# A transformer layer's prologue: the first modulation part computed in columns, its loads and the bias table moved

## The reference

```python
mod = jax.nn.silu(c) @ w_ada[l] + b_ada[l]                 # c: (1, 1024), w_ada: (1024, 6144)
sh1, sc1, g1, sh2, sc2, g2 = jnp.split(mod, 6, axis=-1)
h = rmsnorm(x, pre_mix_gain[l]) * (1.0 + sc1[:, None]) + sh1[:, None]
y = token_mixer(h, w_in[l], ...)                           # proj = h @ w_in, w_in: (1024, 3072)
x = x + g1[:, None] * rmsnorm(y, post_mix_gain[l])
h = rmsnorm(x, pre_ffn_gain[l]) * (1.0 + sc2[:, None]) + sh2[:, None]
y = hier_moe(h, ...)                                       # 32 SwiGLU experts, two of them for each token
x = x + g2[:, None] * rmsnorm(y, post_ffn_gain[l])
```

## Time and profile before

| | us |
|---|---|
| Median of 3 runs | 787.15 (783.61 to 787.57) |
| The profiled execution: its own time | 786.79 |
| Its span in the profile | 785.1 |
| PE busy | 732.4 (93%) |
| DVE busy | 637.0 (81%) |
| ACT busy | 526.9 (67%) |
| HBM read | 248.30 MB, 318 GB/s over the span |

### The profile page before, as it was taken

How to read it: one execution, slowest core, us unless ns; L and a number is a source line. 1 busy time by engine, 2 the same in 40 slices (tenths; PEclk the granted TensorE clock), 3 DMA queues, 4 the chain that set the end, 5 groups by cost and what they waited for, 6 DMA issues and landing times.

```text
span 785.1 us, 12664 instructions
## 1 busy us (share of the span) xinstructions
PE 732.4 (93%) x4733; PEld 572.3 (73%) x4734; DVE 637.0 (81%) x539; ACT 526.9 (67%) x546; POOL 307.3 (39%) x214
## 2 busy tenths in 40 slices
PE   4769999989769999999999999999999999999994
PEld 1248577544557888888888888888888888888883
DVE  3364285645647999999999999999999999999995
ACT  2020133365526888888888888888888888888873
POOL 7400000040053444666444666444666544666000
PEclk9979999999658999999999999999999999999998
DMA  9999987720518899999999999999999999999901
GB/s 342 327 406 385 393 317 281 286 92 0 214 55 299 301 372 374 379 371 369 373 368 385 373 376 377 365 382 374 371 377 366 375 374 381 374 372 375 365 1 57
DMA packets 101997, 249.69 MB, mean 318 GB/s; under 512 B 8134, under 2 KB 8146, under 8 KB 98898
## 3 DMA queue, kind: packets, MB, share of 16 engines
q1 hardware_dynamic: 96448, 244.33, 84.1%
q10 hardware_dynamic: 5092, 3.46, 1.4%
q0 software_dynamic: 432, 1.59, 0.6%
HBM read 248.30 MB, written 1.07 MB: 318 GB/s over the span
## 4 chain that ended last, share of the span: by engine, by line
PE 85%; DVE 6%; DMA 4%; POOL 2%; ACT 2%; issue 1%; DVEq 0%; ACTq 0%; POOLq 0%
PE PS L1294 46%; PE PS L1282 7%; PE PS L1262 7%; PE PS L1253 6%; PE PS L1086 5%; PE PS L1204 4%; PE PS L1080 4%; POOL line L380 2%; DMA toe<-line_dram 2%; PE PS L1272 2%; DMA tabT<-in_rel_bias_dram 1%; DVE MOD L726 1%; PE PS L1061 1%; DMA line_dram<-line 1%; DVE S L802 1%
## 5 line engine op out<-in xcount | busy, mean ns | idle before, releaser
L946 DVE TENSOR_TENSOR WL<-W,WH 128x2048 fp32r<-128x2048 f32 x187 | 419.8, 2295 | 7.3 <-ACT WH L629 7.3
L629 ACT CAST WH<-W 128x2048 fp32r<-128x2048 f32 x187 | 349.9, 1904 | 48.5 <-PE PS L1294 48.5
L423 POOL TENSOR_SCALAR OG<-slot_no,cur 128x128 f32<-128x128 f32 x64 | 161.7, 2530 | 0.0
L1294 PE MATMUL PS<-WH,XT 128*128 128x512 f32 x512 | 139.9, 395 | 0.6 <-DVE XT L965 0.6
L1294 PE MATMUL PS<-WL,XT 128*128 128x512 f32 x508 | 139.9, 397 | 0.0
L410 POOL COPY cur<-PG 128x4 f32 (+1 forms) x33 | 8.3, 251 | 275.7 <-PE PS L1272 228.2
L1294 PEld LDWEIGHTS PS<-WH,XT 128*128 128x128 f32 x512 | 96.7, 189 | 23.6 <-DVE XT L965 0.6
L1294 PEld LDWEIGHTS PS<-WL,XT 128*128 128x128 f32 x508 | 96.0, 189 | 22.4
L420 POOL TENSOR_SCALAR OH<-slot_no,cur 128x128 bf16<-128x128 f32 x64 | 106.6, 1675 | 0.0
L726 DVE SCALAR_TENSOR_TENSOR MOD<-W,cS,MOD 128x2048 f32<-128x2048 f32 x20 | 47.0, 2349 | 29.6 <-DMA W<-in_w_ada_dram 29.3
L1294 PE MATMUL PS<-WH,HT 128*128 128x512 f32 x248 | 69.2, 401 | 1.5 <-issue 1.5
(11 more groups left out here) (198 smaller groups left out, 778.5 us busy)
## 6 DMA issues: line engine op xcount, KB each, us to landing
W<-in_w_gate_dram SPq DMA_DIRECT2D x64, 1024.0 KB, 8.0
W<-in_w_down_dram SPq DMA_DIRECT2D x64, 1024.0 KB, 6.0
W<-in_w_up_dram SPq DMA_DIRECT2D x63, 1024.0 KB, 9.9
W<-in_w_ada_dram SPq DMA_DIRECT2D x24, 1024.0 KB, 8.3
W<-in_w_in_dram SPq DMA_DIRECT2D x12, 1024.0 KB, 13.9
W<-in_w_out_dram SPq DMA_DIRECT2D x4, 1024.0 KB, 11.4
toe<-line_dram POOLq DMA_DIRECT2D x1, 1536.0 KB, 13.4
X<-in_x_dram ACTq DMA_DIRECT2D x1, 1024.0 KB, 12.4
```

The lines of the kernel that those rows point to most:

```text
L423: nc.gpsimd.tensor_scalar(OG[:, buf, t, :], slot_no[:], cur[:, buf, 0, t:t + 1], cur[:, buf, 1, t:t + 1], ALU.is_equal, ALU.mult).then_inc ...
L629: nc.scalar.copy(WH[:, (UPE * odd + u) % SPLITS, :], source).then_inc(hi_ready, 1)
L946: nc.vector.tensor_tensor(low, source, WH[:, (UPE * odd + u) % SPLITS, :].bitcast(f32), ALU.subtract).then_inc(lo_ready, 1)
L1294: last = nc.tensor.matmul(PS[:, bank, :], lhsT, w[:, q * 512:(q + 1) * 512], start=begin, stop=end)
```

## The change

The first modulation part is loaded as 8 other units ("first", part, j): four with the 1024 scale columns (rows 256j to 256j+255, two row blocks side by side), then four with the 1024 shift columns. All four units of the projection's blocks 0 and 1 follow sooner: no later modulation units stand ahead of block 0, two stand between blocks 1 and 2, behind them come three, three, four and four.

The results of the first part are kept in columns: `scol` and `shcol` hold one value for each of 8x128 channels, in the partition of the channel. DVE multiplies 1024 columns at a time (`first`). The sum over the partitions is made on PE with a piece of 128 columns of `MOD` as weights and one column of ones moving (`add_rows`). The biases, the condition and the gain come as 8 rows of 128 values, and PE turns them to columns against the identity matrix; the biases do this in the PSUM bank into which the sums are then added. PE takes the second scale unit (row blocks 2 and 3) as weights, with one column of silu(c) moving (16 products). The rows of x are only scaled by their inverse norm, on ACT. PE transposes them, and scale and shift are applied when `hT` is written, four of eight pieces on ACT and four on DVE. The first projection block runs over the lower four row blocks for all columns first and then over the upper four, in four PSUM banks. The last shift multiplication is cut into four pieces.

The bias line is built in the other order and `toe` is read backwards by DVE, so the flips, their copies and the flipping matrix go. The load of `toe` waits for block 1's second unit. The three gain rows and the router's loads are issued by ACT behind its four copies of blocks 0 and 1, no longer ahead of them. The 16 later `ada` operations are spread over DVE's attention in another way: 5 ahead of `scores(0)`, 11 behind it.

```diff
-    units = [("ada", 0, k) for k in range(DC)]
+    units = [("first", part, j) for part in (1, 0) for j in range(DC // 2)]
     ada2 = [("ada", a, k) for a in (1, 2) for k in range(DC)]
+    between = (0, 2, 3, 3, 4, 4)
     for b in range(6):
         units += [("win", b, 0), ("win", b, 1)]
-        n = 3 if b < 4 else 2
-        units += ada2[:n]
-        ada2 = ada2[n:]
+        units += ada2[:between[b]]
+        ada2 = ada2[between[b]:]
...
+        CHUNKS = 4
+        ON_TENSOR = (2, 3)
...
-            pool.wait_ge(unit_in[DC - 2], 16)
+            pool.wait_ge(unit_in[slot_of(UNIT_AT["win", 1, 1])], 16)
...
-                act.dma_start(gain[:, 0, :], broadcast(pre_mix_gain, D)).then_inc(pre_gain_in, 16)
...
+            for t in range(TT):
+                act.wait_ge(stat_inv, t + 1)
+                nc.scalar.mul(Hn[:, t, :], X[:, t, :], st[:, 48 + t:49 + t]).then_inc(h_ready, 1)
+
+            act.wait_ge(xT_mm, 2 * TT)
+            act.wait_ge(scale_ready, 1)
+            for chunk in (0, 2):
+                act.wait_ge(shift_mm, chunk + 1)
+                nc.scalar.copy(shcol[:, 2 * chunk:2 * chunk + 2], PS[:, chunk, 0:2]).then_inc(shift_ready, 1)
+                act.wait_ge(shift_ready, chunk // 2 + 1)
+                for k in (2 * chunk, 2 * chunk + 1):
+                    nc.scalar.activation(hT[:, k, :], PS[:, 4 + chunk, (k % 2) * SEQ:(k % 2 + 1) * SEQ], ACT.Identity,
+                                         bias=shcol[:, k:k + 1], scale=scol[:, k:k + 1]).then_inc(hT_act, 1)
...
             for k in range(DC):
+                if k not in ON_TENSOR:
+                    first(1, k, 0, D)
...
+            first(0, 0, 0, D)
             inverse(0)
             inverse(1)
+            first(0, 1, 0, D)
+            dve.wait_ge(scale_mm, 1)
+            dve.wait_ge(gcol_ready, 1)
+            nc.vector.scalar_tensor_tensor(scol[:], PS[:, 2, 0:DC], 1.0, gcols[:], ALU.add, ALU.mult).then_inc(scale_ready, 1)
+            for k in range(2, DC - 1):
+                first(0, k, 0, D)
+            for chunk in range(CHUNKS):
+                first(0, DC - 1, chunk * (D // CHUNKS), (chunk + 1) * (D // CHUNKS))
...
-                for t, cols, j in ((0, slice(0, P), slice(P, 2 * P)), (1, slice(P, 3 * P), slice(0, 2 * P))):
+                for t, cols, j in ((0, slice(0, P), slice(P - 1, None, -1)), (1, slice(P, 3 * P), slice(2 * P - 1, None, -1))):
...
             scores(0)
-            ada(FIRST_ADA + 9)
+            ada(5)
+            ada(6)
             probabilities(0)
             for g in range(1, 5):
                 if g == 1:
-                    ada(FIRST_ADA + 10)
+                    ada(7)
                 scores(g)
-                ada(FIRST_ADA + 10 + g)
+                ada(6 + 2 * g)
+                if g < 4:
+                    ada(7 + 2 * g)
                 probabilities(g)
             scores(5)
-            ada(FIRST_ADA + 15)
+            ada(15)
...
+            pe.wait_ge(first_used, first_done(1, DC // 2 - 1))
+            for k in range(DC):
+                last = add_rows(PS[:, 2, k:k + 1], 1, k)
+            last.then_inc(scale_mm, 1)
...
+            for chunk in range(CHUNKS):
+                pe.wait_ge(first_used, first_done(0, DC // 2 - 1) - (CHUNKS - 1 - chunk))
+                for j in range(2):
+                    last = add_rows(PS[:, chunk, j:j + 1], 0, 2 * chunk + j)
+                last.then_inc(shift_mm, 1)
```

More of the change, by code:

```diff
@@ L50 @@
 UNIT_AT = {u: n for n, u in enumerate(UNITS)}
-def on_tensor(unit):
-    return unit[0] == "ada" and unit[1] == 0 and unit[2] % 2 == 1
-ADA_ORDER = [u for u in UNITS if u[0] == "ada" and not on_tensor(u)]
-FIRST_ADA = DC // 2
+ADA_ORDER = [u for u in UNITS if u[0] == "ada"]
 def slot_of(n):
@@ L212, in projection_bank @@
         def projection_bank(b, half):
-            return 2 * (b % 2) + half if b < 3 else half
+            return 4 + half if b == 1 else half
         def value_bank(g):
@@ L315, in _ @@
                     sp.wait_ge(unit_in[n - AHEAD], 16)
-                if kind == "ada":
+                if kind == "first":
+                    load(n, w_ada[0].rearrange("(j two p) f -> j p two f", two=2, p=P)[b][:, :, a * D:(a + 1) * D])
+                elif kind == "ada":
                     load(n, w_ada[0, b * P:(b + 1) * P, a * UW:(a + 1) * UW].rearrange("p (k f) -> p k f", k=1))
@@ L528, in _ @@
                 act.dma_start(hgain[:], diff_head_gain.rearrange("l d -> d l")).then_inc(hgain_in, 16)
+            projection(0)
+            projection(1)
+            projection(2)
+            projection(3)
+            with nc.allow_non_contiguous_dma(reason="small columns"):
                 act.dma_start(gain[:, 1, :], broadcast(post_mix_gain, D)).then_inc(gain_in, 16)
@@ L1069, in _, with add_rows @@
-            pe.wait_ge(hT_ready, 4)
+            def add_rows(out, part, k):
+                return nc.tensor.matmul(out, MOD[:, part * D + k * P:part * D + (k + 1) * P], ones[:, 0:1],
+                                        start=False, stop=True, skip_group_check=True)
+            pe.wait_ge(ada_b_in, 32)
+            nc.tensor.matmul(PS[:, 2, 0:DC], scaleR, ident[0:DC, 0:DC], start=True, stop=True)
+            pe.wait_ge(c_silu, 1)
+            for k in ON_TENSOR:
+                at = UNIT_AT["first", 1, k // 2]
+                pe.wait_ge(unit_in[slot_of(at)], 16)
+                for col in range(DC):
+                    nc.tensor.matmul(PS[:, 2, col:col + 1], W[slot_of(at)][:, (k % 2) * D + col * P:(k % 2) * D + (col + 1) * P], cS[:, k:k + 1],
+                                     start=False, stop=True, skip_group_check=True)
```

182 lines of the change are left out of this document (95 added, 87 removed).

## The result

The changed kernel takes 779.01 us (median of 7 runs, 777.64 to 780.13). Beside it the kernel before took 786.97 us (median of 7, 782.38 to 787.57). The ratio is 0.9918, 95% interval 0.9893 to 0.9943, which is 4.5 to 8.4 us less. That is faster by more than 0.5%. The forecast was 775.3 us with a range of 769 to 784, and the measured median lies in that range, 3.7 us above the forecast.

The account below looks back on a forecast made before the run. Up to `score(0)` PE's late start was taken as the bound, behind `toe`'s load and the flips, then PE's stalls. 786.8 - 19.0 (earlier `score(0)`) + 5.9 (extra `ada`) + 1.6 (ACT's hold) = 775.3 us, range 769 to 784.

Parts of the forecast that it names:

- Last shift unit landed: Loads ahead of the projection: 31.57 before, 1.4 us sooner without the spread gain row, so landing at 30.2.
- First product of the projection: Projection's start: 30.2 plus DVE's shift work, column products and `hT` writes gives 34.4, bounds 32.5 to 36.0.
- Half clock in block 0: PE at the projection's start: half clock after little work and a wait, a loss of 2.1 us.
- ACT's issues end: ACT's queue: seven small loads from 65.0, over at 80.8 by the copied duration or 76.7 with 640 packets gone.
- Cost of ACT's hold: ACT's issues delaying block 2's copies, `scores(0)` and block 3: between 0 and 3.2 us, the middle taken, 1.6.
- Extra `ada`, with the clock behind PE's waits: DVE in the attention: one more `ada` for each of groups 0 to 3, 4.7 + 0.15 + 1.1 = 5.9 us.
- Its own range of 771.5 to 779: Whole kernel: range around 775.3 from the bounds of the start, the clock and ACT's hold.
- Taking away the flips alone would find the modulation right behind it: Before the projection: modulation done at 43.91, 1.6 us before the flips began, so it would be next in the way.
- The split of the block hides it: Projection block 0: its second unit comes 3.8 us later, hidden by 7 us of PE work on the first half.
- Rival 4: DVE in the attention: reading `toe` backwards costs its double, 780 us; chance 0.08.
- Rival 5: Before `scores(0)`: `toe` lands late behind 8 KB packets, after 93.5, making the kernel slower than before, 791 at 98; chance 0.03.
- Rival 2: ACT's queue: small packets alternate with 8 KB weights, hold ends at 84 to 87, 778.5 to 782 us; chance 0.16.

Follow-up runs that it names:

- changed_again: The changed kernel run once more, unaltered, in a later group: 779.57 us, ratio 0.9925 to the kernel before.
- adas_late: Changed kernel with the four extra `ada` moved from groups 0 to 3 to just ahead of group 4's scores: 773.33 us, ratio 0.9849.
- units_as_before: Changed kernel with the later modulation units spread among the projection's as in the kernel before, three behind block 0: 787.46 us, ratio 1.0029.
- loads_on_sp: Changed kernel with the three gain and four router loads issued by SP behind `w_out`'s last unit, not by ACT: 774.07 us, ratio 0.9864.
- loads_early: Changed kernel with the seven gain and router loads issued by ACT ahead of its copies of blocks 0 and 1: 775.73 us, ratio 0.9891.
- pe_kept_busy: Changed kernel with two unread products of 512 columns added on PE ahead of the projection's start: 778.79 us, ratio 0.9929.
- one_more_before_scol: Changed kernel with one shift multiplication moved ahead of DVE's wait for the scale sums: 779.24 us, ratio 0.9917.
- flips_alone: Kernel before with only the bias line built in the other order, `toe` read backwards and the flips removed: 777.86 us, ratio 0.9914.
- sp_and_adas: Changed kernel with the seven small loads on SP and the four extra `ada` ahead of group 4's scores: 768.95 us, ratio 0.9792.
- router_on_sp: Changed kernel with only the four router loads moved to SP, the three gain loads staying on ACT: 773.49 us, ratio 0.9849.
- three_in_flight: Changed kernel with the first 12 units loaded three at a time and not two: 777.59 us, ratio 0.9914.
- all_edits: Changed kernel with loads_on_sp, adas_late, one_more_before_scol and three_in_flight together: 765.61 us, ratio 0.9747.

## Why the prediction was right, and where it was not

| Step | Forecast | Kernel after |
|---|---|---|
| Last shift unit landed | 30.2 | 27.64 (31.76 in changed_again) |
| Block 0's lower unit landed | 34.2 | 30.33 |
| First product of the projection | 34.4 (32.5 to 36) | 34.85 (37.13) |
| Half clock in block 0 | 2.1 | 1.95 (2.29) |
| `score(0)` | 78.2 | 78.26 |
| ACT's issues end | 76.7 to 80.8 | 82.22 |
| Cost of ACT's hold | 1.6 | 4.65 |
| Extra `ada`, with the clock behind PE's waits | 5.9 | 7.8 |
| `score(0)` to `score(5)` | 59.4 by the sum (51.9 + 5.9 + 1.6), some 58 by the text | 64.4 (64.6) |
| Experts | no change | 2.7 less |

In the profiled executions the sum closes: 786.79 - 19.0 + 4.65 + 7.8 - 2.7 = 777.5, against 777.64. The 7.8 is what adas_late took away; with the loads moved first, the split is 6.0 and 6.4. The forecast of 775.3 was 2.3 below this execution and 3.7 below the median.

The forecast held its range, and the mechanisms that it named were the ones at work. But it came as near as it did by some luck: two errors in the start cancelled, and 2.7 us of the experts, which no term had, made up for a part of the 5 us by which the attention was priced too low. Its own range of 771.5 to 779 also does not follow from its bounds: added up, they give 769.7 to 781.0.

**The start.** The time was right, two terms of it were not, and they cancelled. I placed the start behind the last landing, plus two operations of DVE and the column products. The landing came 2.6 us sooner, and that of block 0's lower unit 3.9. But DVE still had nine operations in a row in front of it, held up by its wait for the scale sums. The sum had no term for DVE's own queue. They were all there to be counted behind that wait, five of 1.3 us and four pieces. In the executions with slower loads the forecast's mechanism holds, and the start is at 36.2 to 37.1, above my upper end of 36.0.

**The clock.** The size was right: a loss of 1.95 us, where the row with the idle wait for `toe` had given 2.1. By the pace of its products PE had been at the half clock all the while before the start (16 column products took 3.57 us both at 20.19 and at 31.42, 16 transposes 3.65 at 23.62). That fits the weak work in front, which the prediction named first, and not a restart after a wait.

**The flips.** "Taking away the flips alone would find the modulation right behind it" holds by the trace: with the flips gone the modulation is done at 43.45 and the transposes follow it. The prediction left it at that, and a reader would take it for little. It was 7.8 us at the start and 8 in the end: the four flips (eight records) had ended at 51.34, 7.4 us behind the modulation. Reading `toe` backwards costs nothing: two additions take 1.02 us (line 813 at 85.72 above) as they did forwards. Rival 4 is out. Rival 5 is out as well: `toe` was issued at 42.31 and landed 12.8 us later, 30 us before it is wanted. (Four times 13.42 behind 46 would have been 99.7 and not 98, which changes nothing here.)

**Slack of the units.** "The split of the block hides it", and block 1's second unit there by 46 and wanted at 50: true in the changed kernel, where blocks 0 and 1 ran without a gap. How narrow it was, units_as_before shows.

**ACT's hold, the term that was mis-sized.** I took the middle of two values, 0 and 3.2 us. It was 4.65, above both. Both copied the duration of issues behind small packets. The DMA queues of the kernel after, from 68 to 78 us, answer to the earlier trace rows (q1 carries the weights, q10 what ACT issued):

```profile
DMA packets 752, 4.17 MB, mean 417 GB/s; under 512 B 66, under 2 KB 66, under 8 KB 415
...
q1 hardware_dynamic: 383, 2.79, 66.9%
q10 hardware_dynamic: 369, 1.38, 34.6%
```

They still go one for one, 383 packets against 369, as 313 against 311 in the earlier trace rows. But these 383 weigh 7.3 KB each (2.79 MB / 383), and of the 369 some 337 are the gains' 4 KB ones (1.38 MB / 4,096 B); the view counts no more than 66 small packets in both queues. So the queue moved 37 packets in a us and not the 156 of the earlier trace rows. I had divided 640 packets by 156 and taken the 4 us off the hold. At 37 a us the packets that still had to leave took four times as long each, and that used up what the 640 sent ahead had saved. Rival 2 named this mechanism, with the hold ending at 84 to 87. The end was 82.22, between the forecast's upper value (80.8) and that. Put into the prediction's own step the measured end gives the measured cost: 82.22 - 78.26 + 0.6 = 4.6. By the same step rival 2's ends would have cost 6.4 to 9.4 and given 780.1 to 783.1 us, not the 778.5 to 782 that it states, so that the time of 779.01 falls into its range is in part an error of arithmetic. Its mechanism had 0.16 and should have been the forecast: nothing in the trace spoke for the pace of small packets behind 8 KB ones.
The rule of the Trainium skill that the prediction named (DMA: Bandwidth & Descriptors, "Queues, rings and completion order") has each engine go round between queues at packet granularity. The counts here agree, one for one, as the profile counts packets.

**The extra ada.** The waits ahead of the transposes were there (2.20, 2.95 and 1.23 us; forecast near 3 and 3 for the first two), and the four operations cost 5.9 by their durations. Not in the sum was the clock. The wait of 3.80 us was followed by a half of 8.83 us in place of 7.07, which is hidden, since PE waits for DVE behind it. The one of 2.95 was followed by 8.52, and the 1.45 us of that count in full. Of the 1.9 us between 7.8 and 5.9 that leaves 0.45 without a name.

**The experts.** Not touched by the change, yet 556.0 us against 558.7. The timeline of PE at their entry, first in the kernel after, then in the kernel before:

```profile
224.04 1.20 PE L1359 MATMUL PS<-WH,XT 128*128 128x512 f32 x4 [0.67 <-DVE XT L999]
225.07 1.09 PE L1359 MATMUL PS<-WL,XT 128*128 128x512 f32 x4
```

```profile
230.68 2.05 PE L1294 MATMUL PS<-WH,XT 128*128 128x512 f32 x4 [0.57 <-DVE XT L965]
232.53 1.83 PE L1294 MATMUL PS<-WL,XT 128*128 128x512 f32 x4
```

The same products behind nearly the same wait run at the full clock in one and at half in the other. Among the 14 profiles they run full in seven (the kernel after, changed_again, loads_on_sp, loads_early, pe_kept_busy, one_more_before_scol, units_as_before) and half in seven (the kernel before, flips_alone, adas_late, sp_and_adas, router_on_sp, three_in_flight, all_edits). From the first of them to the end of the span it is 551.0 to 551.9 us in the first seven and 552.9 to 554.6 in the others. So both states occur with the changed prologue, and the 2.7 us between one pair of profiles can't be booked to the change. The wait does not decide it (0.57 us in both groups); what does is open.

## What to carry to other kernels

When an edit moves the start of a stretch that is bound by PE, go through every queue that lay beside it and ask what is issued in it and who stands behind that: ACT's hold was free while PE had 28 us of products beside it, and one of 17.6 us cost 4.7 when it began 13.6 us ahead of `score(0)`. Count a DMA issue by its packets and by the size of the packets it takes turns with, not by its bytes: 144 KB in 2048 packets held the engine, 1.6 MB in 384 did not. Filler work that shares an engine with the path belongs where that engine is idle (10.1 us ahead of group 4) and not spread evenly, and a wait of PE can be charged twice: those of 2.4 to 4.2 us here were mostly followed by 1.3 to 2.6 us of loss to the half clock. Not all were: in loads_early the half behind a wait of 3.35 us took its 7.07. And take the parts of a large change one at a time: here the smallest part alone gave all that the whole did.

## What the runs showed of the hardware that was not expected

**An issue seems to wait for packets to leave.** The issue of `w_expert` ended when about the same number of packets of ACT's queue was left: 3072 issued by then and 961 sent in the kernel before (queue q10, from 53 us to the issue's end at 67.74) leave 2111; 3072 and 1004 in flips_alone leave 2068; 2432 and 306 in the kernel after leave 2126; 2432 and 305 in adas_late leave 2127; 2432 and 246 in units_as_before leave 2186; 2432 and 331 in changed_again leave 2101. The issue itself took between 4.50 and 13.27 us in these six. loads_early fits less well: its issue took 14.33 us, and 3072 and 1133 leave 1939. These are counts over windows and not a limit read anywhere, and no run was made to test it.

**The pace of the loads differs between executions.** With two 1 MB units in flight one landed each 2.6 us in the kernel after (25.08, 27.64, 30.33, 33.04 in SP's queue), and the last shift unit of the same code came 4.47 us behind the one before it in changed_again (27.29 and 31.76). With a deep queue and packets of weights alone it was 407 GB/s over 26 us (loads_on_sp, 64 to 90).

**In the kernel before, the mean clock of an execution goes with its time.** Of 30 executions of the kernel before, the ten with a mean granted clock of 0.972 or more took 779.8 to 782.9 us, the fourteen with 0.967 or less took 783.5 to 789.6. In changed_again and flips_alone, with six runs each, no such order is seen, and the mean counts the time ahead of a trace's first clock record as full speed. A difference of 3 us in one pair of profiles is therefore no result.
